# Output projections and the first two up panels worked one token block at a time, with four more conditioning panels summed on VectorE

## What is computed

```python
def sqrelu_mlp(h, w1, w2):
    return jnp.square(jax.nn.relu(h @ w1)) @ w2

cond = jax.nn.silu(c)
for l in range(DEPTH):
    ada = cond @ ada_w[l] + ada_b[l]
    sh1, sc1, g1, sh2, sc2, g2 = jnp.split(ada, 6, axis=-1)
    ...
    x = x + g1[:, None, :] * rmsnorm(y, norm_g[l, 1])
    h = modulate(rmsnorm(x, norm_g[l, 2]), sh2, sc2)
    y = sqrelu_mlp(h, mlp_w1[l], mlp_w2[l])
    x = x + g2[:, None, :] * rmsnorm(y, norm_g[l, 3])
```

## Time and profile before

| | us |
|---|---|
| median of 3 runs | 1060.33 (1058.5 to 1061.13) |
| span of the profiled execution | 1060.4 |
| output projection wo_c begins | 530.9 |
| first up matmul of MLP 0 | 567.4 |
| end of MLP 0 on TensorE | 748.0 |
| output projection wo_d begins | 836.5 |
| first up matmul of MLP 1 | 870.3 |

### The profile page before, as it was taken

How to read it: one execution, slowest core, us unless ns; L and a number is a source line. 1 busy time by engine, 2 the same in 40 slices (tenths; PEclk the granted TensorE clock), 3 DMA queues, 4 the chain that set the end, 5 groups by cost and what they waited for, 6 DMA issues and landing times.

```text
span 1060.4 us, 19777 instructions
## 1 busy us (share of the span) xinstructions
PE 1011.3 (95%) x8530; PEld 879.9 (83%) x8530; DVE 724.9 (68%) x1194; ACT 531.2 (50%) x804; POOL 36.4 (3%) x33
## 2 busy tenths in 40 slices
PE   5999999889999999999999999999989899999997
PEld 4788899886888887887687999998678769999995
DVE  6789889518989776745766577665778765444544
ACT  3358432225734594563545555445646656445452
POOL 0000044100000100000000000000000000000000
PEclk9999999989999999999999999999989999999998
DMA  9664410432484452653445867777456266455420
GB/s 382 238 278 159 159 42 4 194 130 80 159 317 170 173 214 92 263 202 139 177 167 191 348 250 269 303 301 290 186 226 250 81 238 237 160 199 198 160 80 40
DMA packets 15223, 205.42 MB, mean 194 GB/s; under 512 B 1816, under 2 KB 1816, under 8 KB 2976
## 3 DMA queue, kind: packets, MB, share of 16 engines
q1 hardware_dynamic: 14544, 202.55, 50.3%
q10 hardware_dynamic: 592, 1.61, 0.5%
HBM read 203.10 MB, written 1.05 MB: 193 GB/s over the span
## 4 chain that ended last, share of the span: by engine, by line
PE 84%; DVE 10%; ACT 3%; issue 2%; DMA 1%; SPq 0%; DVEq 0%; ACTq 0%
PE bank L452 20%; PE bank L454 20%; PE bank L453 20%; PE bank L755 5%; PE bank L401 4%; DVE slot_parts L1910 2%; PE bank L658 1%; PE bank L559 1%; DVE arena L2387 1%; PE bank L736 1%; PE bank L631 1%; DVE arena L2375 1%; DMA pc<-in_params 1%; PE bank L620 1%; DVE arena L1853 1%
## 5 line engine op out<-in xcount | busy, mean ns | idle before, releaser
L452 PE MATMUL bank<-page_parts 128*128 128x512 f32 (+2 forms) x1254 | 430.4, 343 | 7.2 <-DVE page_parts L2193 2.3
L1910 DVE TENSOR_TENSOR slot_parts<-ring,page_parts 128x2048 fp32r<-128x2048 f32 (+2 forms) x121 | 271.4, 2254 | 139.0 <-ACT page_parts L1306 138.3
L1306 ACT ACTIVATE page_parts<-ring 128x2048 fp32r<-128x2048 f32 (+2 forms) x121 | 226.8, 1885 | 147.1 <-PE bank L454 91.2
L452 PEld LDWEIGHTS bank<-page_parts 128*128 128x128 f32 x1254 | 238.9, 191 | 34.1 <-issue 6.1
L454 PE MATMUL bank<-page_parts 128*128 128x512 f32 (+2 forms) x686 | 266.7, 389 | 0.0
L453 PE MATMUL bank<-slot_parts,page_parts 128*128 128x512 f32 (+2 forms) x686 | 266.6, 389 | 0.0
L453 PE MATMUL bank<-page_parts 128*128 128x256 f32 x568 | 160.7, 283 | 0.0
L454 PE MATMUL bank<-page_parts,slot_parts 128*128 128x256 f32 x568 | 160.7, 283 | 0.0
L454 PEld LDWEIGHTS bank<-page_parts 128*128 128x128 f32 x686 | 129.7, 189 | 26.5
L453 PEld LDWEIGHTS bank<-slot_parts,page_parts 128*128 128x128 f32 x686 | 130.0, 190 | 24.7
L1363 ACT ACTIVATE arena<-bank 128x512 f32<-128x512 f32 (+2 forms) x134 | 74.2, 575 | 131.7 <-PE bank L454 70.8
(11 more groups left out here) (298 smaller groups left out, 1147.9 us busy)
## 6 DMA issues: line engine op xcount, KB each, us to landing
ring<-in_stream SPq DMA_DIRECT2D x95, 2048.0 KB, 8.5
arena<-in_x SPq DMA_DIRECT2D x2, 512.0 KB, 4.3
arena<-in_gn ACTq DMA_DIRECT2D x2, 512.0 KB, 4.6
out<-arena SPq DMA_DIRECT2D x2, 512.0 KB, 2.6
cc<-in_consts SPq DMA_DIRECT2D x1, 899.0 KB, 6.5
small<-in_cond ACTq DMA_DIRECT2D x1, 512.0 KB, 10.0
pc<-in_params SPq DMA_DIRECT2D x1, 287.0 KB, 6.8
arena<-in_head_sel ACTq DMA_DIRECT2D x1, 32.0 KB
```

Of the source, the lines that this page charges most:

```text
L452: mm(out, a[0], b[0], start=start, stop=False)
L1306: act(unit_parts(n)[0], unit_values(n)[1], ACT.Copy).then_inc(ac.step("w_hi"), 1)
L1910: tt(unit_parts(n)[1], lo, hi, ALU.subtract).then_inc(dv.step("w_lo"), 1)
```

## The change

- The output projections `wo_c` and `wo_d` are worked by token block: all four units for block 0, then all four for block 1 (`split_blocks`, in which the wait is now given by the caller, for each k).
- The norms, the addition to X, the transposes and the splits are made for each block by itself (`post_norm_block`, `norm_block`, `y_block`, `x_block_squares`, `scaled_rows`, `split_rows`). Block 0's transposes stand in front of the last unit of block 1's projection.
- up0 and up1 are worked by token block too (`up_rows`), with the activations as the stationary operand and 512 columns: 48 matmuls for a panel. Their result has tokens in the rows, so after the ReLU it is transposed back (`turn_up`, four transposes for each of the four pieces), squared and split. The order starts up0, up1, down0, up2 as before.
- The four `ada_direct` panels around the output projections and their four turns go; these panels are summed on VectorE inside the MLPs, nine in MLP 0 (seven before) and two in MLP 1 (none before). Where they stand in the stream is set by `ada_before_up` and `ada_before_down`, and after which unit a quarter is summed by `ada_quarters`, counted from up0's first unit as 0.
- The gate of MLP 0 (`spread(1)`) moves from between the two projection panels to the sixth round of the MLP. Six pages take turns for the high parts instead of three.

The diff, cut to its core:

```diff
-        HKV_PAGES, HB_PAGES, MLSTM_PAGES, MLP_PAGES = (16, 15, 16), (12, 11, 12), (8, 5, 7), (8, 5, 8)
-        AF_HI, AF_LO = (arena_parts[n][:, :].rearrange("p (a k t) -> p a k t", a=2, k=4) for n in (6, 9))
+        HKV_PAGES, HB_PAGES, MLSTM_PAGES, MLP_PAGES = (16, 15, 16), (12, 11, 12), (8, 5, 7), (8, 6, 8)
+        AF_HI, AF_LO = (arena_parts[n][:, :].rearrange("p (a k t) -> p a k t", a=2, k=4) for n in (5, 9))
         RL = page(10, 2).rearrange("p a (k t) -> p a k t", k=4)
+        RL_ROWS = page(10, 4)
+        MLP_UNITS = (4, 14, 2, 11, 3, 12)
...
-        ada_units = (tuple(range(1, 8)), ())
+        ada_before_up = (range(3, 9), range(3, 4))
+        ada_before_down = ((1, 2, 4), (2,))
+        ada_quarters = ({u: 2 if u in (4, 5, 8, 9, 14, 15, 16, 17, 30, 31) else 1 for u in range(4, 32) if u not in (6, 7)},
+                        {8: 2, 9: 2, 10: 1, 11: 1, 12: 1, 13: 1})
...
-            def mlp(l):
+            def from_first(*pages):
+
+                n = len(units) % len(pages)
+                return pages[-n:] + pages[:-n] if n else pages
+
+            def mlp(l, branch, src, wait, beside):
 
                 stage[0] = f"mlp{l}"
-                pe.wait_ge(sem("xn"), 8 + 4 * l)
-                transposes(f"hT_m{l}", XN)
-                ada_turned()
-                rotation["banks"] = [4, 5, 6, 7]
+                rotation["banks"], rotation["at"] = [4, 5, 6, 7], 0
+                turned = f"hT_m{l}"
+
+                def turn_rows(tb):
+                    turn_block(turned, XN, tb, lambda g: (sem("xn"), 7 + 4 * l + tb))
+
+                def beside_branch(tb, n):
+
+                    beside(tb, n)
+                    if (tb, n) == (1, 3):
+                        turn_rows(0)
+
+                split_blocks(branch, src, from_first(15, 16, 3, 12), lambda tb, k: (sem(wait), k // 2 + 1), beside_branch, (0, 1, 2, 3))
...
+                def up_rows(n, tb, i):
+
+                    if tb == i == 0:
+                        split_panel(("up", l, n), mlp_pages(), by_k=True)
+                        rows_panel[n] = order[-1]
+                    if i == 0:
+                        claim(("up_rows", l, n, tb), n if tb == 0 else None)
+                    u = first + 2 * n + i
+                    W = use_unit() if tb == 0 else unit_parts(u)
+                    if n == 0:
+                        pe.wait_ge(sem(turned + "_split"), 2 * tb + i + 1)
+                    for k in range(4 * i, 4 * i + 4):
+                        ins = three(bank(("up_rows", l, n, tb))[:, :], [a[:, k, tb * P:(tb + 1) * P] for a in h],
+                                    [w[:, k - 4 * i, :] for w in W], k == 0, k == KT - 1)
+                    if i:
+                        ins.then_inc(filled(("up_rows", l, n, tb)), 1)
+                    elif tb:
+                        ins.then_inc(pn.step(), 1)
+                    if tb:
+                        units[u]["used"] = rows_panel[n][1] = pn.last
+
+                def turn_up(n, tb):
+
+                    b = claim(("up_T", l, n, tb))
+                    pe.wait_ge(*evacuated(("up_rows", l, n, tb)))
+                    for k in range(4):
+                        ins = nc.tensor.transpose(b[:, k * P:(k + 1) * P], RL_ROWS[:, 2 * n + tb, k * P:(k + 1) * P], ident)
+                    ins.then_inc(filled(("up_T", l, n, tb)), 1)
...
-                    pe.wait_ge(sem("relu2"), 2 * (8 * l + n) + 2)
+                    pe.wait_ge(sem("relu2"), 16 * l + (2 * n + 2 if n else 3))
                     A = AF_HI[:, n % 2], AF_LO[:, n % 2]
                     for half in range(2):
+                        if n == 0 and half:
+                            turn_up(1, 1)
...
+                up_rows(0, 0, 0)
+                up_rows(0, 0, 1)
+                up_rows(1, 0, 0)
+                turn_rows(1)
+                up_rows(1, 0, 1)
+                turn_up(0, 0)
+                up_rows(0, 1, 0)
+                up_rows(0, 1, 1)
+                turn_up(1, 0)
+                up_rows(1, 1, 0)
+                turn_up(0, 1)
+                up_rows(1, 1, 1)
+                for n in range(1, 9):
+                    if n in ada_before_up[l]:
+                        ada(1)
+                    if 1 < n < 8:
                         up(n)
-                        if n == 0:
-                            ada_turned()
-                        if n in ada_units[l]:
-                            ada(1)
-                        if (l, n) == (1, 6):
-                            spread(3)
-                    if n:
-                        down(n - 1)
+                    if n in ada_before_down[l]:
+                        ada(1)
+                    if n == 6:
+                        spread(1 + 2 * l)
+                    down(n - 1)
...
-            stage[0] = "mlp0"
-            for half in range(2):
-                split_tok(("wo_c", half), split_parts(H2_PAGES), first_of(15, 16, 3), wait=("h2T_split", 0) if half == 0 else None)
-                if half == 0:
-                    spread(1)
-                    ada_turned()
-            ada_direct()
-            split_panel(("up", 0, 0), (3, 4, 14))
-            ada_direct((sem("x_sq"), 7))
-            mlp(0)
+            mlp(0, "wo_c", split_parts(H2_PAGES), "h2T_split", lambda tb, n: ada_turned() if (tb, n) == (0, 2) else None)
...
+                y_block(branch, 0)
+                split(first + 2)
+                x_block_squares(0)
+                scaled_rows(0)
+                y_block(branch, 1)
+                split(first + 3)
+                x_block_squares(1)
+                relu_rows(0, 0)
+                split(first + 4)
+                scaled_rows(1)
+                split(first + 5)
+                relu_rows(1, 0)
+                squares_rows(0, 0)
+                relu_rows(0, 1)
+                squares_rows(1, 0)
+                squares_rows(0, 1)
+                relu_rows(1, 1)
+                split(first + 6)
+                squares_rows(1, 1)
+                split(first + 7)
...
+                        ada(ada_quarters[l].get(n - unit_of["up", l, 0], 0))
...
+            def post_norm_block(i, branch, tb):
...
+                split(first + 1)
+                post_norm_block(2 * l, branch, 0)
+                for q in range(2):
+                    split_quarter(first + 2, q)
+                norm_block(0)
+                for q in range(2, 4):
+                    split_quarter(first + 2, q)
+                split_rows(0)
+                post_norm_block(2 * l, branch, 1)
+                for q in range(2):
+                    split_quarter(first + 3, q)
+                norm_block(1)
+                for q in range(2, 4):
+                    split_quarter(first + 3, q)
+                split_rows(1)
+                split(first + 4)
+                low_rows(1, 0, 0)
+                split(first + 5)
+                low_rows(2, 1, 0)
+                low_rows(3, 0, 1)
+                split(first + 6)
+                low_rows(4, 1, 1)
+                split(first + 7)
...
-            split(unit_of["wo_c", 0] + 1)
-            modulation(6, 12, (1,))
-            gate_diagonal(1)
             split(unit_of["wo_c", 1] + 1)
-            gate_row(1)
-            split(unit_of["up", 0, 0, 0])
-            post_norm(0, lambda half, tb: ("wo_c", half, tb))
-            norm()
-            mlp(0)
+            modulation(6, 10, (1,))
+            mlp(0, "wo_c")
```

More of the change, by code:

```diff
@@ L498, in split_tok, with split_blocks @@
                     ins.then_inc(unit_used((*name, 1) if i else None), 1)
-            def split_blocks(name, src, pages, split, between=None):
+            def split_blocks(name, src, pages, ready, between=None, banks_of=None):
                 first, panels_of = len(units), []
@@ L506, in split_blocks @@
                 for tb in range(TB):
-                    bs = [claim((name, half, tb)) for half in range(2)]
+                    bs = [claim((name, half, tb), None if banks_of is None else banks_of[2 * tb + half]) for half in range(2)]
                     for n in range(4):
@@ L1220, in _ @@
             transposes("o3T", O3, ready=lambda i: evacuated(("at3", "O", i)))
-            stage[0] = "mlp1"
-            for half in range(2):
-                split_tok(("wo_d", half), split_parts(O3_PAGES), first_of(15, 16, 3), wait=("o3T_split", 0) if half == 0 else None)
-            ada_direct()
-            split_panel(("up", 1, 0), (3, 4, 14))
-            ada_direct((sem("x_sq"), 11))
-            mlp(1)
+            mlp(1, "wo_d", split_parts(O3_PAGES), "o3T_split", lambda tb, n: None)
         @block.sync
@@ L1729, in _ @@
             h_squares(MH - 1)
-            page_used.update({p: finished(("num", MH - 1)) for p in (3, 4, 14)})
+            page_used.update({p: finished(("num", MH - 1)) for p in (3, 4, 12, 14)})
             split(unit_of["wo_c", 0] + AHEAD)
@@ L1739, in _ @@
             warm_root()
-            y_squares(lambda half, tb: ("wo_c", half, tb))
```

(37 more changed lines are left out.)

123 lines of the change are left out of this document (89 added, 34 removed).

## The result

The changed kernel takes 1068.7 us (median of 13 runs, 1063.5 to 1071.8), the kernel before 1061.1 (13 runs, 1057.0 to 1065.4). The ratio is 1.0063, 95% interval 1.0048 to 1.0078: slower by some 7 us. The profiled execution has a span of 1067.7 us against 1060.4.

What follows compares the result with a forecast made beforehand. TensorE was taken as the bound, busy 95% of the span and throughout both MLPs. From 1060.4, entries gain 15.3, waits inside the MLPs cost 16.6 (net +1.3) and clock falls +6: 1067.7 us, likeliest single case 1067, range 1055 to 1073.

Steps and rivals of the forecast that it cites:

- the likeliest case: Whole kernel: slower by more than 0.3%, above 1063.5 us, chance 0.6.
- The waits of the ring: Inside the MLPs: TensorE waits for panels whose slots are released late, 15.0 us in MLP 0 and 1.6 in MLP 1.
- 12 if the quick landing holds each time: MLP 0: the waits for panels total 12 us instead of 15.0 if every transfer lands quickly.
- rival 3: Every long gap brings a full 3.3 us clock fall, 1071.7; transfers also slowing each other 0.6 us per wait, 1076; chance 0.15.
- The clock: MLP 0's three 3.4 us gaps: two clock falls at about 3 us each, +6 us, bounds 0 and 10.
- One sign that was named: Profile after the change: PEclk below 9 in one to three slices of MLP 0.
- The entries: From each output projection into its MLP: gains of 5.4 us in MLP 0 and 9.9 in MLP 1, together 15.3.
- The two terms of this gain: MLP 0's entry: 10.2 us net work off TensorE, against new waits of 4.8 us together.
- The ring copes: MLP 0: units split earlier, so up4, up6, up7 and down7 lose their 11.8 us of waits; 1050 us, chance 0.2.
- the point that was given for it: MLP 0, fourth quarter's end: a chain shorter by 3.4 us than 20.1; quarters ending under 5 us after a half would refute the forecast.
- The clock holds: MLP 0: the waits come without clock falls; 1061.7 us, or 1058.7 with quick landings; chance 0.2.

Runs made afterwards that it cites:

- quarters alone: Changed kernel with one table edited: each summed conditioning panel of MLP 0 has its quarters behind two units, two each, instead of one behind each of four; 1054.7 us.
- gaps filled: Changed kernel plus 46 matmuls without use, put ahead of up3, up4, up6 and down7 where TensorE waits; 1068.4 us.
- late quarters: Kernel before, with one quarter of a summed panel behind each of 28 units of MLP 0 instead of two behind each down unit; 1083.9 us.
- and alone: MLP 1 and its output projection in the new form, MLP 0 and wo_c as in the kernel before; 1052.6 us.
- in better places: Kernel with only MLP 1 in the new form, its two summed panels moved behind up2 and up3, two quarters behind a unit; 1052.3 us.
- best stream: Changed kernel with conditioning panels of both MLPs moved, none between MLP 0's last two down panels, and two quarters behind a unit everywhere; 1048.9 us.
- other places: Changed kernel with MLP 0's conditioning panels behind up1 to up4, ahead of up5 to up7 and behind up6's and up7's rounds, two quarters behind a unit; 1053.3 us.

## Why the prediction was right

It said 1067 (1055 to 1073), by a sum of 1067.7 for the profiled execution, and slower by over 0.3% as the likeliest case. That case came, by the mechanism that was named. That the sum hit to 1 us is luck, for the terms of the clock and of MLP 0's entry were each off and cancelled. Step by step:

**The waits of the ring** carried the sum and held: 15.0 us expected in MLP 0, 14.8 measured, each put down to VectorE's low part as foretold. One by one: up3 1.6 and measured 2.6; up4 3.4 and 3.2; up5 1.6 and 1.6; up6 3.4 and 3.1; up7 1.6 and 1.4; down7 3.4 and 2.8; MLP 1's up3 1.6 and 1.7. The one that was off is up3. Its transfer took 9.1 us and not 8.0. The next transfer was issued 2.6 us behind it, but so it was in the two other kernels in which up3 takes up2's slot, and there the transfer took 8.7 (quarters alone) and 8.1 us (gaps filled); the cause of this spread is open. The prediction had it on the quick side ("12 if the quick landing holds each time") and for the slow side in rival 3 alone. That 12 does not come out of its own terms either: three waits of 2.9, one of 1.1 and two of 1.6 are 13.0. And each wait cost 0.24 us more than itself, which the sum had not: a panel ahead of a wait lasts 11.07 instead of 10.91 us without the wait, and one behind it, at full clock, 11.59 instead of 11.51, since a matmul lasts 0.39 us at a pace of 0.23 and overlaps only with one that follows at once. Six waits make 1.4 us, in the changed kernel and in the one with the late quarters.

**The clock** held in its sum by luck, and not in its parts. Two falls at 3 us were expected, and there were four at 1.5 us, ahead of up3, up4, up6 and down7: every wait over 2 us brought one. The slow stretches of 3.4 us in MLP 0 are half as long as the 6.8 us one from which the price was taken, and that row itself is no constant: the same gap of 2.2 us behind MLP 0 has a slow stretch of 6.8 us in five of the nine profiles, of 3.4 in three, and none in one. Chance and price were each off by a factor of two, in opposite directions. One sign that was named failed with it: no slice of MLP 0 has PEclk below 9, because a stretch of 3.4 us is too short to show in a slice of 26.7. The Trainium skill (TensorE: Matmul & The Clock Gate, section "HAM oscillation") tells of a kernel that started slow after every wait for a transfer. The changed kernel's trace agrees for its four waits over 2 us in MLP 0, though not for those of 1.4 and 1.6; the waits of 2.26 and 2.68 us in two other kernels do not agree.

**The entries.** MLP 1: 9.9 gained less 1.6 was expected for its stretch, and 8.3 is what it gained, in the changed kernel and alone. MLP 0: 5.4 expected, 6.0 measured. From the turn ahead of wo_c to up2's first matmul the kernel before takes 72.4 us and the changed one 64.7, and 1.8 of the difference is the gate, which was moved from here to the sixth round, where it lasts 1.7. The two terms of this gain were both off. The waits were 3.3 us and not 4.8: the second unit 1.3 instead of 2.5, since TensorE itself came 0.8 later there for a bank that ScalarE still read, block 0's turn 1.2 instead of 1.6, and none at the first down panel. The work saved was some 9.3 us and not 10.2. So the 16.2 us that wo_c and MLP 0 lost are 14.8 of waits, 1.4 beside them and 5.9 of clock, less 6.0 at the entry (16.1 in these rounded terms).

**Not foreseen** was the stretch behind MLP 0, +1.7 us. Which slot a panel takes was asked of the MLP's panels and not of the first one behind them, q_a's. The start of the changed stretch, 2.3 us earlier in the profiled execution, is chance: in nine profiles it lies between 527.8 and 532.0 us, and the instructions ahead of it are the same in number.

**The rivals.** "The ring copes" (1050) failed at the point that was given for it: the fourth quarter ended 7.2 us behind the half, as in the earlier trace rows. But its number is near what kernels with earlier quarters measured: 1054.7 with the old stream, and 1048.9 with the stream in order as well. "The clock holds" (1061.7) is what the filled gaps should have given, and did not: the wait ahead of up5 grew by 1.7 us and brought a fall, behind a transfer whose slowness is unexplained, and 4 us more passed ahead of wo_c.

What the change is worth, then: 8.4 us in MLP 1 as it stands, 10.1 with its panels in better places (224.0 against 213.9). In MLP 0 it is 2.3 in the best stream (217.9 against 215.7), whose nine panels leave two waits of 3.0 us in all; with the other places it is 3.6 (214.3), but 3.2 of that go again in the longer pause behind it (11.9 instead of 8.7). The loss of 16 us there came not from taking panels off TensorE, but from when their quarters are summed and where they stand.

## What to carry to other kernels

In a ring whose slots are released in order, find for every panel the one four places back (the ring's depth), the instruction that releases it, and the work that lies between that release and the panel's first use; here a panel needs 12.5 us. A step with little work, such as a sum that may be put anywhere, is placed by when it frees its slot, not by when its result is wanted. Whoever lengthens the list must look past its end: the first panel behind it is moved as well. And where an engine is called the releaser of a wait, look at its own idle time first: 9 us stood ahead of the low part of up4.

## What the runs showed of the hardware

- A gap on TensorE may halve its clock or not, and its length alone does not decide. No gap of up to 1.96 us in an MLP brought a fall in the profiles. With 2.26 (quarters alone) and 2.68 us (before, late quarters) there was none, with 2.27 (the same kernel) and 2.62 there was one, and so with all from 2.83 to 3.32 in MLP 0; the pause of 2.90 us behind it had one in one kernel and none in another. The kernel with the quarters alone, whose longest gap in MLP 0 is 2.3 us, spreads from 1051 to 1059 us, with mean clocks from 0.994 to 0.983.
- A fall of 3.4 us costs 1.5 us in dense work (an up panel 13.1 instead of 11.6 us). 46 useless matmuls kept the clock up over four gaps, but the kernel with them measured 1068.4 us against 1068.7: nothing gained.
- A transfer of 2 MB lands 7.5 to 9.1 us after its issue when no other panel's transfer is under way (median 8.1 of 167 in the nine traces, from 300 us on), and 8.1 as well in the median when the next is issued 2 to 4 us behind it (57, up to 9.5). Of two issued within 0.5 us the second lands after 12.2 us or more, median 12.6 (87).
